# Retrieval activations during the choice of experts, and gates through a DRAM table

## The reference, cut to what matters

```python
q = (xt @ w_q).reshape(t, 8, 2, 128)
sc = einsum("thpc,hpnc->thpn", q, sub_keys)            # 2 x 128 key scores a head
top_s, top_i = top_k(sc, 16)
cand_s = top_s[:, :, 0, :, None] + top_s[:, :, 1, None, :]   # 256 pairs a head
cand_i = top_i[:, :, 0, :, None] * 128 + top_i[:, :, 1, None, :]
best_s, best_pos = top_k(cand_s, 16)
idx  = take_along_axis(cand_i, best_pos)
gate = softmax(best_s)
act = einsum("cd,ced->ce", xc, u[idx])
out = einsum("ce,ced->cd", gelu(act) * gate, v[idx])
```

## Time and profile before

| | us |
|---|---|
| median of 3 runs (2686.96 to 2688.36) | 2687.83 |
| the profiled execution | 2685.31 |
| its span | 2683.5 |
| first stages, to the norm before the keys | 311 |
| key scores, 311 to 386 | 75 |
| choice on DVE, 386 to 473.6 | 87.6 |
| gates of blocks 0 to 63, 473.6 to 567 | 93.4 |
| blocks 0 to 63, 567 to 932 | 365 |
| gates of blocks 64 to 127, 932 to 1027.3 | 95.3 |
| blocks 64 to 127, 1027.3 to 1392.4 | 365.1 |
| modulation, sum over partitions, 1392.4 to 1403 | 10.6 |
| all that follows (second block) | 1280.5 |

### The profile page before, as it was taken

One profiled execution on the slowest core, in us unless ns is written; L12 is line 12 of the kernel. 1 busy time (PEld: TensorE's weight loads), 2 busy tenths in 40 slices (PEclk: granted clock), 3 DMA queues, 4 the chain that ended last, 5 costly groups with the idle time before them and its releaser, 6 DMA issues. The chain is left out here.

```text
span 2683.5 us, 36526 instructions
## 1 busy us (share of the span) xinstructions
PE 2294.1 (85%) x14410; PEld 2054.6 (77%) x14410; DVE 1713.8 (64%) x2586; ACT 1212.9 (45%) x1741; POOL 347.7 (13%) x203
## 2 busy tenths in 40 slices
PE   5969760999999999999996857556999999999992
PEld 5947660999999899999975837455888888888881
DVE  3443289766666676666646456555777777777774
ACT  3321220145544424444454521212777777777771
POOL 0000000000000000000000002000344444444440
PEclk9956885579999958999998968786999999999996
DMA  6400420036655603565642400122777777776774
GB/s 231 173 0 32 149 95 0 1 110 220 235 218 209 233 1 126 207 238 216 224 167 94 153 5 1 37 76 91 273 267 283 265 277 279 270 281 261 275 269 151
DMA packets 72098, 449.08 MB, mean 167 GB/s; under 512 B 14385, under 2 KB 14705, under 8 KB 20337
## 3 DMA queue, kind: packets, MB, share of 16 engines
q1 hardware_dynamic: 57600, 419.46, 42.2%
q10 hardware_dynamic: 5106, 18.81, 1.9%
q0 software_dynamic: 9216, 8.42, 1.0%
HBM read 437.12 MB, written 34.67 MB: 176 GB/s over the span
## 5 line engine op out<-in xcount | busy, mean ns | idle before, releaser
L897 PEld LDWEIGHTS ps<-htr,wr 128*128 128x128 f32 x3072 | 389.3, 193 | 11.6
L897 PE MATMUL ps<-htr,wr 128*128 128x256 f32 x3072 | 392.5, 284 | 0.0
L908 PE MATMUL ps<-wr,hgr 128*128 128x512 f32 x1536 | 378.7, 395 | 0.0
L908 PEld LDWEIGHTS ps<-wr,hgr 128*128 128x128 f32 x1536 | 279.3, 188 | 58.5
L1901 DVE TENSOR_TENSOR wr<-big,wr 128x1024 fp32r<-128x1024 f32 x220 | 264.5, 1234 | 86.0 <-ACT wr L1895 86.0
L2059 POOL TENSOR_SCALAR pr<-big 128x128 fp32r<-128x128 f32 x128 | 262.7, 2057 | 190.0 <-issue 167.6
L1913 PE MATMUL ps<-pr,htr 128*128 128x128 f32 x2048 | 244.6, 278 | 3.8 <-POOL pr L2059 3.8
L1913 PEld LDWEIGHTS ps<-pr,htr 128*128 128x128 f32 x2048 | 237.0, 194 | 4.7 <-POOL pr L2059 4.7
L1901 DVE TENSOR_TENSOR wx<-big,wx 128x1024 fp32r<-128x1024 f32 x164 | 197.7, 1232 | 66.7 <-ACT wx L1895 66.6
L1370 POOL TENSOR_TENSOR mix<-big,mix 128x1024 f32<-128x1024 f32 x7 | 18.2, 2594 | 1662.9 <-ACT mix L1358 1662.9
L1895 ACT ACTIVATE wr<-big 128x1024 fp32r<-128x1024 f32 x220 | 224.2, 1062 | 0.7 <-DMA big<-in_wd 0.7
(11 more groups left out here) (376 smaller groups left out, 3123.4 us busy)
## 6 DMA issues: line engine op xcount, KB each, us to landing
big<-in_peer SPq DMA_DIRECT2D x128, 1024.0 KB, 4.9
big<-in_wgu SPq DMA_DIRECT2D x128, 1024.0 KB, 4.9
big<-in_wd SPq DMA_DIRECT2D x64, 1024.0 KB, 4.8
big<-in_w_in SPq DMA_DIRECT2D x33, 1024.0 KB, 4.8
big<-in_w_ada SPq DMA_DIRECT2D x24, 1024.0 KB, 4.7
big<-in_w_out SPq DMA_DIRECT2D x8, 1024.0 KB, 4.9
big<-in_w_q SPq DMA_DIRECT2D x8, 1024.0 KB, 4.8
big<-yscratch ACTq DMA_DIRECT2D x8, 1024.0 KB, 7.0
```

What stands on the lines that cost most here:

```text
L897: inst = T.e.matmul(bank(4 + i % 4)[:, 0:256], w[:, x, k * 128:(k + 1) * 128], HTR0[:, y, k, :], start=k == 0 and p_ == 0, stop=k == 7 and ...
L908: inst = T.e.matmul(bank(2 * t_ + c), HGR[:, i % 2, x, t_ * 128:(t_ + 1) * 128], w[:, y, c * 512:(c + 1) * 512], start=i == 0 and p_ == 0, ...
```

## The change

What it does:

- **The loop is reordered.** `seq` lists the half-blocks: u of blocks 0 to 95 first, then v 0, u 96, v 1, u 97, ... v 31, u 127, and v 32 to v 127 alone. All activations after gelu are kept in SBUF (`ACTS`, 96 blocks; blocks 96 to 127 take the places of v blocks that are done). Units of the ring now hold two u halves or two v halves of 4 KB rows each.
- **The choice is split in four groups** (4 heads by 128 tokens). DVE chooses groups 0 and 1 (heads 0 to 3) before its part of the loop. The rest (`rest()`, 50 steps) is taken one step per half-block, beside the splits, from half-block 6 on. The gates of groups 2 and 3 are ready at half-block 57. Four exponentials stand on ACT between gelus. There is no fence any more between `keys` and `peer`, and the choice is not turned over by PE.
- **The one-hot products are gone** (L821 to L855). POOL zeroes a 16 MB table in DRAM (16 DMAs of 1 MB, after `w_in`), then adds each gate at (expert, token) with 256 indirect DMAs, each 128 elements of 4 bytes, in batches of 16 that wait for the batch before on the same tokens. When all have landed, POOL loads the table block pair by block pair, 256 KB each, into two buffers (`GSH`).
- **Work changes engine.** The rests of `w_q` and of the first eight u halves are taken by POOL. A `w_ada` unit is now scaled in place by ACT (L940) and added by POOL (L1048); the units stand between v pairs from pair 31 on, three for every four pairs (eight v blocks). POOL clears `MOD` at pair 30.

```diff
+        NA, POOLED = 96, 8
+        seq = [("u", i) for i in range(NA)]
+        for i in range(128):
+            seq.append(("v", i))
+            if NA + i < 128:
+                seq.append(("u", NA + i))
...
-        unit(("peer", 0), I["peer"][0], ("v lo", 1))
...
+        for m in range(64):
+            unit(("v", m), I["peer"][2 * m:2 * m + 2, :, 1024:2048].rearrange("a p n -> p a n"), half_done("v", 2 * m + 1))
+            if 48 + m < 64:
+                u_unit(48 + m)
+            for n in range(len(ada)):
+                if 31 + (4 * n) // 3 == m:
+                    ada_after.setdefault(m, []).append(n)
+                    unit(("w_ada", n), I["w_ada"][ada[n][0], ada[n][1]], ("mod part", n + 1))
...
+        def keys_G(G):
+
+            for j in range(8):
+                u, n = LIN["w_q"] + j, at[("w_q", j)]
+                landed(G, n)
+                for i in range(2):
+                    G.wait_ge("lin hi", 2 * u + i + 1)
+                    G.step(G.e.tensor_tensor(WR0[:, 2 * (u % 2) + i, 1, :], placed(n)[:, i * 1024:(i + 1) * 1024],
+                                             WR0[:, 2 * (u % 2) + i, 0, :].bitcast(F32), ALU.subtract), "query lo")
+            for q in range(POOLED):
...
+        def half_A(A, q):
+            landed(A, at[(seq[q][0], seq[q][1] // 2)])
+            if q < 4:
+                A.wait_ge("lin mm", LIN["w_q"] + (7 if q < 2 else 8))
+            else:
+                A.wait_ge("p used", q - 3)
+            A.step(A.e.activation(pair_of(q)[:, 0, :], raw_of(q), ACT.Copy), "p hi")
...
         def peer_A(A):
...
+            for q, (kind, i) in enumerate(seq):
+                if q + 2 < len(seq):
+                    half_A(A, q + 2)
+                if q + 1 < len(seq) and seq[q + 1][0] == "v":
+                    v = seq[q + 1][1]
+                    A.wait_ge("hid", v + 1)
+                    if v >= 2:
+                        A.wait_ge("p used", seq_at[("v", v - 2)] + 1)
+                    A.step(A.e.activation(HGR[:, v % 2, 0, :], acts_of(v), ACT.Copy), "hid hi")
+                if kind == "v" and i % 2 and i // 2 in ada_after:
+                    A.last()
+                    for n in ada_after[i // 2]:
+                        landed(A, at[("w_ada", n)])
+                        A.step(A.e.activation(placed(at[("w_ada", n)]), placed(at[("w_ada", n)]), ACT.Copy,
+                                              scale=CA_[:, ada[n][0]:ada[n][0] + 1]), "mod term")
...
+            for q in range(2):
+                half_V(V, q)
+            for q, (kind, i) in enumerate(seq):
+                if q + 2 < len(seq):
+                    half_V(V, q + 2)
+                if q == 57:
+                    for _ in choosing:
+                        pass
+                    for g in range(2, 4):
+                        gates_V(V, g)
+                elif q + 2 >= POOLED:
+                    next(choosing, None)
+                if q + 2 < len(seq) and seq[q + 2][0] == "v":
+                    v = seq[q + 2][1]
+                    V.wait_ge("gelu", v + 1)
+                    V.wait_ge(f"gates block {v // 2 % 2}", 16 * (v // 4 + 1))
+                    V.step(V.e.tensor_tensor(acts_of(v), acts_of(v), GSH[:, v // 2 % 2, v % 2, :], ALU.mult), "hid")
...
+        def peer_G(G):
+            G.wait_ge("zeroed", 256)
+            for q in range(2):
+                for h in range(4):
+                    for t_ in range(2):
+                        g = 2 * q + t_
+                        if h == 0:
+                            G.wait_ge("gates", g + 1)
+                        if q or h:
+                            G.wait_ge(f"scatter share {t_}", 256 * (4 * q + h))
+                        for k in range(16 * h, 16 * h + 16):
+                            G.e.indirect_dma_start(shares, bass.IndirectOffsetOnAxis(ap=EIX[:, g, k:k + 1], axis=0),
+                                                   GV_[:, g, k:k + 1], None,
+                                                   compute_op=ALU.add).then_inc(s(f"scatter share {t_}"), 16)
+            for t_ in range(2):
+                G.wait_ge(f"scatter share {t_}", 2048)
+            by_block = shares.rearrange("(i j t) o -> i j (t o)", j=128, t=256)
+            for m in range(66):
+                if 2 <= m < 64:
+                    G.wait_ge("hid", 2 * m - 2)
+                if m < 64:
+                    G.e.dma_start(GSH[:, m % 2, :, :], by_block[2 * m:2 * m + 2].rearrange("i j t -> j i t")
+                                  ).then_inc(s(f"gates block {m % 2}"), 16)
...
+                for n in ada_after.get(m - 2, ()):
+                    j = ada[n][1]
+                    o = MOD[:, j * 2048:(j + 1) * 2048]
+                    G.wait_ge("mod term", n + 1)
+                    G.last()
+                    G.step(G.e.tensor_tensor(o, o, placed(at[("w_ada", n)]), ALU.add), "mod part")
```

500 lines of the change are left out of this document (224 added, 276 removed).

## The result

| | before | after |
|---|---|---|
| median, us | 2688.1 (2686.96 to 2689.06) | 2810.53 (2802.41 to 2811.92) |
| profiled execution | 2685.31 | 2802.41 |
| its span | 2683.5 | 2800.5 |
| last key product to the end of the modulation sum | 1017 | 1134 |
| what follows | 1280.5 | 1278.4 |

The change makes the kernel slower: ratio 1.0449 of the medians, 95% interval 1.0429 to 1.047. The forecast was 2552 us with a range from 2460 to 2690; its rival "the adding DMA costs more than the copying one, and the kernel gets slower" came true.

The account below looks back on a forecast made before the run. PE was taken to bound the loop and one-hot stretches, DVE the choice between them. 705.5 + 2.4 + 450.2 + 98 = 1256, plus 10.5 is 1267 instead of 1403: gain 136 us, forecast 2552, range 2460 to 2690.

Parts of the forecast that it names:

- the adding DMA costs more than the copying one, and the kernel gets slower: POOL's queue from 411 to the first block pair: above 1.65 us per DMA slower, 2778 us at 2.0; chance 0.17.
- What bounds the kernel, what goes: Loop and one-hot stretches PE-bound, choice DVE-bound; removing 188.7 us of one-hot products and 87.5 of waiting: ceiling 276 us.
- the choice does not hide: Choice steps beside the rests take 3.2 us instead of 2.87, PE loses 16 us: 2568 us; chance 0.05.
- Start of the loop: POOL takes the rests of `w_q`; only the first unit is late, 4 to 5 us, PE starts `acts(0)` at 391.
- u stretch: 96 u blocks at 2.87 us are 275.5 us on PE, from 391 to 666.5, with the choice hidden.
- The gates' path: Choice, 256 adding DMAs, first load and splits set the first `outs` at 705.5; PE waits 39 us from 666.5.
- 256 x 1.09 us: POOL's scatter: each adding DMA spaced 1.09 us like a copying one, 139.5 us per half of 128.
- The pause between the halves: POOL's scatter: first half done at 550.5, second half waits for half-block 57 until 558.
- v stretch, first part: PE's work of 128 x 2.80 + 32 x 2.87 = 450.2 us, with DVE, ACT and loads keeping up.
- v stretch with the modulation: From pair 31 on `w_ada` units hold ring slots 16.9 us against 12.8: 24 x 4.1 = 98 us lost.
- the second term: Modulation part: DVE held by POOL's product needs 6.7 us a pair against PE's 5.6, 34 us; not added.
- The sum: Modulation sum done at 1267 where it was 1403: gain 136 us, profiled execution 2549, median 2552 us.

Follow-up runs that it names:

- the two cheap repairs: Changed kernel, still adding, with the modulation product back on DVE and the rests of the u stretch in four parts: 2705.43 us, ratio 1.0058 to before.

## Why the prediction was wrong, step by step

- **What bounds the kernel, what goes: right.** With the scatter taken out the kernel runs at 2504.55 us, and nothing else holds PE at 671. The choice is hidden in full; the rival "the choice does not hide" is out.
- **Start of the loop: right.** Forecast 391, measured 388.5.
- **u stretch: nearly right.** Forecast 275.5 us to 666.5, measured 282.5 to 671, with PE 279.5 busy. The clock is 0.99 and there are short gaps: 0.6 us for POOL's first rests, 2.0 us where DVE waits for the second exponential on ACT, 0.4 later.
- **The gates' path: the step that failed.** The term "256 x 1.09 us" was mis-sized twice. The start was right (forecast 411, measured 413.2).
  - *The price of an add, taken from a copy.* "I take 1.09, the row it is nearest to": that row was a copying DMA, and the step took adding to be a matter for the DMA engines, whose cost it put at 0.42 us. That is what an add shows (0.41), though partly by luck, since the copying DMAs it came from had large elements. But the add is also dearer on POOL, 1.55 + 0.30 against 0.96 + 0.30 us. 256 x (1.86 - 1.09) = 197 us.
  - *DVE beside it.* "DVE beside it does not stretch it" rested on the earlier trace rows, where POOL's DMA starts 0.27 us before DVE's product. What decides is the opposite order, and the earlier trace rows had shown, for a POOL product, that the first one holds the other. 78 us.
  - *The pause between the halves*, forecast 7.5 us, went. Sum: 2 + 197 + 78 - 7.5 = 269.5; the first outs came 974.0 - 705.5 = 268.5 us later than forecast.
- **v stretch, first part: right.** 186.0 of 186.0 us busy up to 1160, at 2.80 and 2.87 us.
- **v stretch with the modulation: nearly right in size, right in mechanism.** Loss 85.8 us against 98; restart 1.7 against 2.4; SP waits for POOL's sum 24 times, as the forecast said. POOL's sum took 3.81 us (forecast 4.0). "The DMA engines leave no room either" was too strong: transfers account for at most 15 of the 86. And the second term, DVE behind POOL, was rightly not added: DVE's own work is what bounds the part once POOL's is gone.
- **The sum.** 268.5 - 13 in the v stretch - 2 in what follows = 253.5; 2549 + 253.5 = 2802.5, the profiled execution. The median of the four, 2810.5, is 8 us above it, and these are not explained.
- **The rivals.** The first named the mechanism, the place and the break-even, 1.65 us for a DMA, and gave 2778 us for 2.0. Spacing was 1.86 undisturbed and (965.1 - 413.2) / 255 = 2.16 in the mean. Its own formula, 411 + 256 x 2.16 + 2.7 = 967, is 2 us short of the first load's issue at 968.6. Its chance of 0.17 was too low. The estimate that the prediction made with the Trainium skill ("DMA: Bandwidth & Descriptors", Specifications, and "HBM Reference", Latency) gave 1.6 us where POOL's 1.55 was measured, 1.86 with the pause that its sum needed. It counted time of the DMA engines, whose share is 0.22 while POOL is at its limit: the number is near, the mechanism is not shown, and that is luck. The range ended at 2690, since I cut it at the rival's break-even and not at its own bound, 2.0 us, which the text had kept "for the range".
- **How far was the forecast from what the reorder can do?** The version without adds takes 2572.65, 0.8% above 2552, but by another road: its outs start 80 us later than forecast (785.5 against 705.5), and behind pair 31 it loses 38 us instead of 98, since DVE does the modulation. That the totals are so near is luck.

## What to carry to other kernels

A queue of many small indirect DMAs is priced by what one costs its issuing engine, so measure that very form (adding, copying, with its neighbours) before 256 of them are put on the path that a stage waits for; here each 0.1 us was worth 26 us of the kernel. Where an add is only there for duplicates, merging the duplicates on an engine with slack and then copying bought 0.6 us per DMA (outs start 785.5 against 910.3 with the two cheap repairs alone). And where two periodic streams share something, look at the order in which they start: 0.08 us decided over 1.0, and a gap in the middle of DVE's instruction gave nearly all of it back. That holds for the adding DMAs; with copies the same gap gave 5 to 7 us.

## What the runs showed of the hardware that I had not expected

- An indirect DMA that adds takes POOL 1.55 us for 128 elements and 1.42 for 64; one that copies, 0.96 and 0.89. 0.30 us lie between two of them in each case.
- An adding DMA of 128 elements leaves 143 packets in the queue record and one of 64 leaves 77; a copying one to the same places leaves 31, with 128 elements or 64.
- An indirect DMA that starts 0.08 us behind a DVE product with two SBUF inputs takes 2.58 us instead of 1.55; one that starts 0.15 us ahead of it takes 1.55.
- In the trace of one kernel PE fell to one matmul in 2.3 to 2.8 us for some 136 us, with no wait recorded, and its four executions took 2751.67 us in the median; executed on another chip the same kernel ran without it (2586.57 us). The cause is open.
